# A two-layer hybrid decoder trunk on one core: layers written out, first step of each net by token tile, shorter first loads and final norm

## The chip, the core and the metric

The kernel runs on one core of a Trainium2 chip. A core has TensorE (matmuls and transposes, results in PSUM), VectorE (DVE), ScalarE (ACT), GpSimd (POOL) and a queue, SyncE (SP), that here issues nearly all DMAs. Each engine runs its own list of instructions in order and waits on semaphores for the others. The metric is the device time of one execution in microseconds.

## The reference, cut

Two layers over 256 tokens of width 1024, all in float32:

```
for l in range(2):
    x = LN1(ALPHA * x + 0.5 * (silu(x @ w_gate) * (x @ w_up)) @ w_down)   # w_gate, w_up: 1024 x 2816
    x = LN2(ALPHA * x + mixer(x))      # x @ w_in (1024 x 4864), conv, S5 scan, window attention, gates, w_out
    x = LN3(ALPHA * x + 0.5 * SwiGLU_2(x))
```

## The kernel before

All weights, about 200 MB, are read from HBM once in 93 chunks of 1 MB per layer (33 for each feed-forward net, 27 for the mixer). A chunk lands in one of three raw slots (`load`, on SP). ACT rounds it to fp32r (`split`, w_hi, L710), DVE subtracts to get the rest (`rest`, w_lo, L1056), and TensorE multiplies in three passes: hi x hi, hi x lo, lo x hi. Activations are split in the same way. A slot's raw part is free once `rest` is done, and its hi and lo parts when TensorE has used them (semaphore `used`).

The 256 tokens are two tiles of 128. `xtok` holds x by token, `xT` holds it by feature: 8 feature chunks, hi and lo. TensorE keeps PSUM banks 0 to 3 as accumulators (`acc`) of a net's output; tile 0 is in banks 0 and 1, tile 1 in 2 and 3.

A feed-forward net has 11 steps of 256 hidden columns. `project` computes a gate or an up chunk: the weights are stationary, 256 tokens move, 48 matmuls (L426 to L428). ACT applies silu, DVE multiplies (`hid`), both split it, and `accumulate` adds its product with a down chunk: 24 matmuls of 512 columns (L441). Gate and up of step i+1 run ahead of the accumulation of step i. Ahead of the first step `open_acc` writes zeros to the accumulators (L467).

Between two nets stands `norm`. When the accumulators of tile 0 are complete, DVE adds the residual (L1108), takes statistics (L1112, L1117, L1119), POOL raises the variance to -0.5 (L988) and DVE normalises (L1123). The same follows for tile 1. TensorE transposes each tile (L456, 8 transposes), ACT evacuates with gain and shift (L768; for a quarter it is DVE, L1154) and casts to hi (L762), DVE subtracts to get lo (`x_rest`, L1102). Only then can `project` start. At LN1 eight more transposes, of the scan's B and C matrices (L522, L523), stand between the two tiles' transposes, and the first mixer chunk is K/V, which is computed by token tile with x stationary (L543 to L545).

The layers are a hardware loop on every engine (`Fori(0, DEPTH)`). So the input x takes the same path as the output of a layer: gains are set to 1, and x is transposed, evacuated and split like any other. All parameter vectors are loaded by the ACT queue at the start, and SP waits for them before it loads the first weights. Behind the loop DVE and POOL multiply the normalised output by the gain and add the shift (L1442, L1444, L1038, L1040), and two stores write it.

Within an engine the order of the code is the order of the work: no scheduler moves anything.

```
with sp.Fori(0, DEPTH) as l:                       # and so on each engine
norm(l, 1, FFN0[1] - 1, 1.0); turned(l, 1)         # DVE between mixer and second net
rest(l, FFN0[1] + 1)                               # low part of the second weight chunk, behind it
```

## Time and profile before

| | |
|---|---|
| Median of 3 runs | 1194.88 us (1194.86 to 1196.68) |
| Profiled execution | 1195.63 us, span 1193.8 us |
| Busy in the span | TensorE 1145.8 us (96%), DVE 753.7 (63%), ACT 575.2 (48%), POOL 154.1 (13%) |
| Read from HBM | 203.77 MB, 172 GB/s over the span |
| Mean granted TensorE clock | 0.984 |

The span runs from the first to the last instruction. A busy time is a share of it, and says nothing of what waits for what; the timeline does.

### The profile page before, as it was taken

The numbers are of one execution on the slowest core, as the hardware profiler recorded it, in microseconds if no ns is written. First come the engines' busy times: TensorE is split into PE (matmuls) and PEld (weight loads), VectorE is DVE, ScalarE is ACT, GpSimd is POOL, SyncE is SP. The second block draws the span as 40 slices with busy tenths as digits, with TensorE's granted clock in tenths as the row PEclk, the third lists the DMA queues.
The fourth block names the chain that finished last, engine by engine and source line by source line (L and its number), as shares of the span: only waits on it lengthen the run. The fifth ranks groups of instructions, "written<-read, shape, count | busy, mean of one in ns | idle before, by whom it ended". The sixth has DMA issues, their size and how long they took to land.

```text
span 1193.8 us, 20955 instructions
## 1 busy us (share of the span) xinstructions
PE 1145.8 (96%) x8164; PEld 1082.6 (91%) x8166; DVE 753.7 (63%) x700; ACT 575.2 (48%) x652; POOL 154.1 (13%) x147
## 2 busy tenths in 40 slices
PE   5999999999999899999979999999999998999995
PEld 5999999999999799999879999989999988999994
DVE  4665447779948664544557544577897586644455
ACT  5565553863444544334356555455735435334331
POOL 2199000003000000000004950000300000000001
PEclk8999999999999899999989999999999998999998
DMA  7565567443466456556455655645445563555650
GB/s 223 181 211 189 192 200 193 155 129 117 139 178 200 153 177 190 195 176 215 139 157 178 207 176 189 232 107 177 141 135 153 174 219 126 191 178 187 197 177 35
DMA packets 176209, 205.60 MB, mean 172 GB/s; under 512 B 27012, under 2 KB 160792, under 8 KB 176152
## 3 DMA queue, kind: packets, MB, share of 16 engines
q1 hardware_dynamic: 175824, 204.76, 54.2%
q8 instruction: 36, 0.59, 0.2%
q14 instruction: 21, 0.17, 0.1%
q10 hardware_dynamic: 328, 0.08, 0.0%
HBM read 203.77 MB, written 1.05 MB: 172 GB/s over the span
## 4 chain that ended last, share of the span: by engine, by line
issue 79%; POOL 13%; PE 6%; ACT 1%; DVE 1%; POOLq 0%; ACTq 0%; DVEq 0%
POOL rot_c L1008 3%; POOL rot_s L1014 2%; POOL tp L1012 2%; POOL S L1022 2%; PE ps L428 1%; PE ps L427 1%; PE ps L426 1%; POOL tp L1010 1%; POOL tp L1004 1%; POOL tp L1006 1%; ACT S L879 1%; PE ps L606 1%; POOL rstd L988 1%; PE ps L543 0%; PE ps L544 0%
## 5 line engine op out<-in xcount | busy, mean ns | idle before, releaser
L1056 DVE TENSOR_TENSOR w_lo<-raw,w_hi 128x2048 fp32r<-128x2048 f32 x186 | 434.4, 2338 | 271.4 <-ACT w_hi L710 271.4
L426 PE MATMUL ps<-xT,w_hi 128*128 128x256 f32 x1984 | 568.1, 286 | 12.8 <-DVE xT L1102 12.8
L427 PE MATMUL ps<-xT,w_hi 128*128 128x256 f32 x1984 | 564.6, 285 | 0.0
L428 PE MATMUL ps<-xT,w_lo 128*128 128x256 f32 x1984 | 564.5, 285 | 0.0
L710 ACT CAST w_hi<-raw 128x2048 fp32r<-128x2048 f32 x186 | 353.4, 1902 | 155.1 <-PE ps L428 114.7
L426 PEld LDWEIGHTS ps<-xT,w_hi 128*128 128x128 f32 x1984 | 384.2, 194 | 17.3 <-DVE xT L1102 15.7
L427 PEld LDWEIGHTS ps<-xT,w_hi 128*128 128x128 f32 x1984 | 384.2, 194 | 1.7
L428 PEld LDWEIGHTS ps<-xT,w_lo 128*128 128x128 f32 x1984 | 383.9, 193 | 0.0
L441 PE MATMUL ps<-w_hi,rows_hi 128*128 128x512 f32 x416 | 130.8, 391 | 0.0
L441 PE MATMUL ps<-w_lo,rows_hi 128*128 128x512 f32 x416 | 130.4, 390 | 0.0
L441 PE MATMUL ps<-w_hi,rows_lo 128*128 128x512 f32 x416 | 130.2, 389 | 0.0
L988 POOL TENSOR_TENSOR rstd<-veps,mhalf 128x1 f32<-128x1 f32 x12 | 6.6, 550 | 815.3 <-DVE veps L1119 815.3
L441 PEld LDWEIGHTS ps<-w_lo,rows_hi 128*128 128x128 f32 x416 | 78.1, 188 | 16.7
L441 PEld LDWEIGHTS ps<-w_hi,rows_lo 128*128 128x128 f32 x416 | 78.1, 188 | 16.6
L721 ACT CAST rows_hi<-hid 128x512 fp32r<-128x512 f32 x44 | 27.3, 620 | 132.3 <-PE ps L441 98.2
L441 PEld LDWEIGHTS ps<-w_hi,rows_hi 128*128 128x128 f32 x416 | 75.3, 189 | 13.1
L715 ACT ACTIVATE act<-ps 128x512 f32<-128x512 f32 x44 | 26.3, 597 | 123.0 <-PE ps L428 122.9
L1069 DVE TENSOR_TENSOR rows_lo<-hid,rows_hi 128x512 fp32r<-128x512 f32 x44 | 32.7, 742 | 57.5 <-ACT rows_hi L721 57.4
L1064 DVE TENSOR_TENSOR hid<-act,ps 128x512 f32<-128x512 f32 x44 | 30.2, 687 | 49.1 <-PE ps L428 49.1
L818 ACT ACTIVATE gates<-ps 128x512 f32<-128x512 f32 x24 | 14.4, 598 | 80.6 <-PE ps L428 80.6
L768 ACT ACTIVATE xTf<-ps,ln_cur 128x128 f32<-128x128 f32 x72 | 27.0, 455 | 9.9 <-PE ps L456 9.9
L1008 POOL TENSOR_TENSOR rot_c<-tp 128x512 f32<-128x512 f32 (+6 forms) x18 | 31.7, 1759 | 1.4
(186 smaller groups left out, 930.4 us busy)
## 6 DMA issues: line engine op xcount, KB each, us to landing
raw<-in_ffn_w_gate SPq DMA_DIRECT2D x44, 1024.0 KB, 5.4
raw<-in_ffn_w_up SPq DMA_DIRECT2D x44, 1024.0 KB, 5.3
raw<-in_ffn_w_down SPq DMA_DIRECT2D x44, 1024.0 KB, 4.9
raw<-in_w_in SPq DMA_DIRECT2D x34, 1024.0 KB, 5.3
raw<-in_w_out SPq DMA_DIRECT2D x8, 1024.0 KB, 4.9
raw<-in_w_in SPq DMA_DIRECT2D x16, 256.0 KB, 4.5
raw<-in_w_br_attn SPq DMA_DIRECT2D x16, 256.0 KB, 4.6
gb<-in_ln_g SPq DMA_DIRECT2D x6, 512.0 KB, 5.3
```

The costliest lines, as they stand in the source:

```text
L426: mm(o, h[:, c, n], xT[:, c, 0, :], start=i == 0, stop=False)
L427: mm(o, h[:, c, n], xT[:, c, 1, :], start=False, stop=False)
L428: last = mm(o, w[:, c, n], xT[:, c, 0, :], start=False, stop=i == KC - 1)
L441: last = mm(acc[:, t, n, :], left[:, buf, c, tok], right[:, c, n * 512:n * 512 + 512], start=start and first and c == 0, stop=stop and lef ...
L710: nc.scalar.copy(w_hi[s][:, :], raw[s][:, :]).then_inc(hi_made.sem, 1)
L715: act_(act[:, :, :], ps[:, 4, :].rearrange("p (m t) -> p m t", m=2), ACT.Silu).then_inc(silu_made.sem, 1)
L721: nc.scalar.copy(rows_hi[:, buf], hid[:, :, :]).then_inc(h_hi.sem, 1)
L768: last = act_(xTf[:, c, t * P:t * P + P], ps[:, 6 - 2 * t + c // 4, (c % 4) * P:(c % 4 + 1) * P], ACT.Identity, scale=ln_cur[:, 2 * (norm_ ...
L1008: tt(rot_c[:, tl, n:2 * n], t0, t1, ALU.subtract).then_inc(pool_chain, 1)
L1056: tt(w_lo[s][:, :], raw[s][:, :], f32(w_hi[s][:, :]), ALU.subtract).then_inc(lo_made.sem, 1)
L1064: tt(hid[:, :, :], act[:, :, :], ps[:, 5, :].rearrange("p (m t) -> p m t", m=2), ALU.mult).then_inc(h_made.sem, 1)
L1069: tt(rows_lo[:, buf], hid[:, :, :], f32(rows_hi[:, buf]), ALU.subtract).then_inc(h_lo.sem, 1)
```

## The change

- Layers are written out in Python loops on every engine; the inner loops over steps stay.
- The first gate and up chunks of each net are computed by token tile with x stationary (`by_token`), into banks 0 and 1 and with tokens as rows: tile 0 by pairs of feature chunks, with tile 1's transposes ahead of tile 0's last pair. The first `hid` is therefore by token, and TensorE transposes it (four transposes). `open_acc` is gone: the first accumulation starts the banks.
- ACT evacuates and casts by pairs of feature chunks, DVE's `x_rest` goes by pairs too, and for tile 0 stands between the residual and statistics operations of tile 1. At the second and third norm the `rest` of the next net's second chunk (`second`) moves from behind the norm to between its tiles; in layer 0 that of the next layer's first chunk goes ahead of the norm.
- The input is cast straight from PSUM, without gains. The first loads are issued at once: tile 0 of x, half of the first weight chunk, tile 1 of x, the other half, the second chunk; the parameter vectors come behind these on SP, and their transposes move into the first net's step 1. Eight zero matmuls run ahead of the first transposes.
- In the last norm DVE does centring times gain, and then times deviation plus shift, in two operations; tile 0 is stored when it is ready, and tile 1 in two halves.

```diff
+first = ffn1_w_gate[0].rearrange("(c p) n -> p c n", p=P)
+sp.dma_start(xtok[:, 0, :], x[0, 0:P, :]).then_inc(x_landed[0], 16)
+sp.dma_start(cols(raw[0])[:, 4:KC, :], first[:, 4:KC, 0:256]).then_inc(first_landed, 16)
+sp.dma_start(xtok[:, 1, :], x[0, P:2 * P, :]).then_inc(x_landed[1], 16)
 sp.sem_inc(lo_made.sem, SLOTS)
 sp.sem_inc(used.sem, SLOTS)
...
-sp.wait_ge(small_landed, 16 * 12)
...
-    load(l, k0, columns(w_gate, l, 0))
+    if l == 0 and f == 0:
+        load(l, k0, lambda r: [(cols(r)[:, 0:4, :], first[:, 0:4, 0:256])])
+    else:
+        load(l, k0, columns(w_gate, l, 0))
...
-with sp.Fori(0, DEPTH) as l:
+for l in range(DEPTH):
...
+def by_token(l, norm, t, p, chunks):
+    pe.wait_ge(x_lo.sem, x_lo.at(l, 8 * norm + 4 * t + p + 1))
+    tok = slice(t * P, t * P + P)
+    for c in PAIRS[p]:
+        for slot, o, inc in chunks:
+            h, w = cols(w_hi[slot])[:, c, :], cols(w_lo[slot])[:, c, :]
+            mm(o, xT[:, c, 0, tok], h, start=c == UPPER_FIRST[0], stop=False, skip_group_check=True)
+            mm(o, xT[:, c, 0, tok], w, start=False, stop=False, skip_group_check=True)
+            last = mm(o, xT[:, c, 1, tok], h, start=False, stop=c == UPPER_FIRST[-1], skip_group_check=True)
+            if inc and c == UPPER_FIRST[-1]:
+                last.then_inc(used.sem, 1)
...
-def open_acc(l, n):
-    pe.wait_ge(res_made.sem, res_made.at(l, n))
+def gate_up_by_token(l, k0, norm):
+    transposes(l, norm, 0)
+    take(l, k0)
+    take(l, k0 + 1)
     for t in range(NT):
-        for h in range(2):
-            mm(acc[:, t, h, :], zero_b[:, 0:P], zero_b[:, :], start=True, stop=False,
-               skip_group_check=True)
+        part = slice(t * 256, t * 256 + 256)
+        chunks = ((0, ps[:, 0, part], t), (1, ps[:, 1, part], t))
+        for p in range(4):
+            if t == 0 and p == 3:
+                transposes(l, norm, 1)
+            by_token(l, norm, t, p, chunks)
+def gate_up_of_input():
+    pe.wait_ge(zero_made, 1)
+    for _ in range(8):
+        mm(ps[:, 1, :], zero_b[:, 0:P], zero_b[:, :], start=True, stop=True, skip_group_check=True)
+    pe.wait_ge(ident_made, 1)
+    transposes(0, -1, 0)
+    pe.wait_ge(first_lo, 1)
+    for k in range(2):
+        for t in range(NT):
+            part = slice(t * 256, t * 256 + 256)
+            for p in range(4):
+                if k == 0 and t == 0 and p == 2:
+                    transposes(0, -1, 1)
+                    take(0, 0)
+                elif k == 1 and t == 0 and p == 0:
+                    take(0, 1)
+                by_token(0, -1, t, p, ((k, ps[:, k, part], t),))
 def ffn(l, f, norm):
     k0, s0 = FFN0[f], f * STEPS
-    take(l, k0)
-    project(0, 4, l, norm)
-    take(l, k0 + 1)
-    project(1, 5)
-    def step(i):
+    if l == 0 and f == 0:
+        gate_up_of_input()
+    else:
+        gate_up_by_token(l, k0, norm)
+    def step(i, first=False):
         take(l, k0 + i * 3 - 1)
-        pe.wait_ge(silu_made.sem, silu_made.at(l, s0 + i))
+        if not first:
+            pe.wait_ge(silu_made.sem, silu_made.at(l, s0 + i))
         project(2, 4)
+        if first and l == 0 and f == 0:
+            pe.wait_ge(rows_made, 1)
+            nc.tensor.transpose(ps[:, 7, 0:N_LN], ln_rows, ident[0:N_LN, 0:N_LN])
+            nc.tensor.transpose(ps[:, 7, P:P + N_SMALL], small_rows, ident[0:N_SMALL, 0:N_SMALL]
+                                ).then_inc(pro_tp, 1)
         take(l, k0 + i * 3)
         pe.wait_ge(h_made.sem, h_made.at(l, s0 + i))
+        if first:
+            for m in range(2):
+                for t in range(NT):
+                    n = m * SEQ + t * P
+                    last = nc.tensor.transpose(ps[:, 6, n:n + P], hid[:, t, m * P:m * P + P], ident[:, :])
+            last.then_inc(hT_done.sem, 1)
         project(0, 5)
         take(l, k0 + i * 3 + 1)
         pe.wait_ge(h_lo.sem, h_lo.at(l, s0 + i))
-    with pe.Fori(1, STEPS - 1) as i:
+    step(1, True)
...
+    step(1, True)
+    accumulate(1, 0, start=True).then_inc(used.sem, 1)
+    with pe.Fori(2, STEPS - 1) as i:
...
+for l in range(DEPTH):
...
+def first_hidden_hi(l, f):
+    sc_.wait_ge(hT_done.sem, hT_done.at(l, f + 1))
+    nc.scalar.copy(rows_hi[:, 0], ps[:, 6, :].rearrange("p (m t) -> p m t", m=2)).then_inc(h_hi.sem, 1)
...
+def norm(l, norm_):
+    def evacuate(t, p, n):
+        for c in PAIRS[p]:
             last = act_(xTf[:, c, t * P:t * P + P], ps[:, 6 - 2 * t + c // 4, (c % 4) * P:(c % 4 + 1) * P],
                         ACT.Identity, scale=ln_cur[:, 2 * (norm_ % 3), c:c + 1],
                         bias=ln_cur[:, 2 * (norm_ % 3) + 1, c:c + 1])
         last.then_inc(xTf_act.sem, 1)
-        sc_.wait_ge(xTf_act.sem, xTf_act.at(l, norm_ * 3 + n))
-        x_split(slice(ks[0], ks[-1] + 1), t)
+        sc_.wait_ge(xTf_act.sem, xTf_act.at(l, norm_ * 6 + n))
+        x_split(slice(PAIRS[p][0], PAIRS[p][1] + 1), t)
     sc_.wait_ge(tp_upper.sem, tp_upper.at(l, norm_ * NT + 1))
-    evacuate(0, range(4, KC), 1)
+    evacuate(0, 0, 1)
+    evacuate(0, 1, 2)
     sc_.wait_ge(tp_made.sem, tp_made.at(l, norm_ * NT + 1))
-    evacuate(0, range(4), 2)
-    if between:
-        between()
+    evacuate(0, 2, 3)
+    evacuate(0, 3, 4)
...
+    cast(0, 1)
+    cast(0, 0)
+    sc_.wait_ge(first_landed, 16)
+    nc.scalar.copy(cols(w_hi[0])[:, 4:KC, :], cols(raw[0])[:, 4:KC, :]).then_inc(first_hi, 1)
+    sc_.wait_ge(landed[0], LANDED[0])
+    nc.scalar.copy(cols(w_hi[0])[:, 0:4, :], cols(raw[0])[:, 0:4, :]).then_inc(hi_made.sem, 1)
+    cast(1, 1)
+    cast(1, 0)
+    split(0, 1)
...
+def x_rest(l, norm_, t, p):
+    dve.wait_ge(x_hi.sem, x_hi.at(l, norm_ * 8 + 4 * t + p + 1))
+    ks, tok = slice(PAIRS[p][0], PAIRS[p][1] + 1), slice(t * P, t * P + P)
     tt(xT[:, ks, 1, tok], xTf[:, ks, tok], f32(xT[:, ks, 0, tok]), ALU.subtract).then_inc(x_lo.sem, 1)
...
+    def centred(t):
+        stt(xtok[:, t, :], xtok[:, t, :], mv[:, t, 0:1], gb[:, 0, :], ALU.subtract, ALU.mult
+            ).then_inc(dev_made, 1)
+        dve.wait_ge(dev_made, t + 1)
+        dve.wait_ge(rstd_made.sem, rstd_made.at(l, norm_ * NT + t + 1))
+    def finished(t, at):
+        stt(xtok[:, t, at], xtok[:, t, at], rstd[:, t:t + 1], gb[:, 1, at], ALU.mult, ALU.add
+            ).then_inc(out_made, 1)
     dve.wait_ge(acc_done.sem, acc_done.at(l, 2 * norm_ + 1))
...
+    if final:
+        dve.wait_ge(gb_landed.sem, gb_landed.at(DEPTH, 0))
+        centred(0)
+        finished(0, slice(0, D))
+    else:
+        normalise(0, slice(0, D))
+    def ahead(p):
+        if not final:
+            x_rest(l, norm_, 0, p)
     dve.wait_ge(acc_done.sem, acc_done.at(l, 2 * norm_ + 2))
+    if second is not None:
+        second()
     residual(1, slice(0, 1)).then_inc(dve_chain, 1)
     dve.wait_ge(dve_chain, links.next())
-    stats(1, 0)
+    if second is None:
+        stats(1, 0)
     dve.wait_ge(used.sem, used.at(l, k + 1))
     residual(1, slice(1, 2)).then_inc(res_made.sem, 1)
     dve.wait_ge(res_made.sem, res_made.at(l, norm_ * NT + 2))
+    ahead(0)
+    if second is not None:
+        stats(1, 0)
+    ahead(1)
     stats(1, 1).then_inc(dve_chain, 1)
+    ahead(2)
     deviation(1)
-    normalise(1, slice(D // 2, D))
-    normalise(1, slice(0, D // 2))
-def turned(l, norm_, between=None):
-    x_rest(l, norm_ * 4 + 1, slice(4, KC), 0)
-    x_rest(l, norm_ * 4 + 2, slice(0, 4), 0)
+    if final:
+        centred(1)
+        finished(1, slice(0, D // 2))
+        finished(1, slice(D // 2, D))
+    else:
+        ahead(3)
+        normalise(1, slice(D // 2, D))
+        normalise(1, slice(0, D // 2))
...
+    low(0, 1)
+    low(0, 0)
+    dve.wait_ge(first_hi, 1)
+    tt(cols(w_lo[0])[:, 4:KC, :], cols(raw[0])[:, 4:KC, :], f32(cols(w_hi[0])[:, 4:KC, :]), ALU.subtract
+       ).then_inc(first_lo, 1)
+    dve.wait_ge(hi_made.sem, hi_made.at(0, 1))
+    tt(cols(w_lo[0])[:, 0:4, :], cols(raw[0])[:, 0:4, :], f32(cols(w_hi[0])[:, 0:4, :]), ALU.subtract
+       ).then_inc(lo_made.sem, 1)
+    low(1, 1)
+    low(1, 0)
+    rest(0, 1)
...
-    norm(l, 1, FFN0[1] - 1, 1.0)
+    norm(l, 1, FFN0[1] - 1, 1.0, lambda: rest(l, FFN0[1] + 1))
     turned(l, 1)
-    rest(l, FFN0[1] + 1)
-    ffn(l, 1, True, lambda: scaled_back(l, 1))
-    norm(l, 2, LAYER_CHUNKS - 1, 0.5)
-    links.leave()
-dve.wait_ge(gb_landed.sem, gb_landed.at(DEPTH, 0))
-dve.wait_ge(xn_made.sem, xn_made.at(DEPTH, 0))
-for t, part in ((1, slice(0, D)), (0, slice(D // 2, D))):
-    tt(xtok[:, t, part], xtok[:, t, part], gb[:, 0, part], ALU.mult).then_inc(dve_chain, 1)
-    dve.wait_ge(dve_chain, links.next())
-    tt(xtok[:, t, part], xtok[:, t, part], gb[:, 1, part], ALU.add).then_inc(out_made[t], 1)
+    ffn(l, 1, lambda: scaled_back(l, 1))
+    if l < DEPTH - 1:
+        rest(l + 1, 0)
+        norm(l, 2, LAYER_CHUNKS - 1, 0.5, lambda: rest(l + 1, 1))
+        turned(l + 1, -1)
+    else:
+        norm(l, 2, LAYER_CHUNKS - 1, 0.5, None, True)
```

What stands in the engines' lists at three places follows. The names are those of the tiles, and "waits" names the semaphores on which an instruction waits.

DVE between mixer and second net, from the statistics of tile 1 on, before:

```order
L1112 BN_STATS bnst<-xtok 128x6 [waits dve_chain]
L1139 REGISTER_ALU
L1108 SCALAR_TENSOR_TENSOR xtok<-xtok,ps 128x512 [waits used]
L1141 REGISTER_ALU
L1112 BN_STATS bnst<-xtok 128x6 [waits res_made]
L1115 REGISTER_ALU
L1117 BN_AGGR mv<-bnst 128x2 [waits dve_chain]
L1118 REGISTER_ALU
L1119 TENSOR_SCALAR veps<-mv 128x1 [waits dve_chain]
L1123 TENSOR_SCALAR xtok<-xtok,mv,rstd 128x512 [waits rstd_made]
L1123 TENSOR_SCALAR xtok<-xtok,mv,rstd 128x512
L1102 TENSOR_TENSOR xT<-xTf,xT 128x4x128 [waits x_hi]
```

and now, from the normalisation of tile 0 on:

```order
L1167 TENSOR_SCALAR xtok<-xtok,mv,rstd 128x1024 [waits rstd_made]
L1095 TENSOR_TENSOR w_lo<-raw,w_hi 128x2048 [waits hi_made,acc_done]
L1152 SCALAR_TENSOR_TENSOR xtok<-xtok,ps 128x512
L1152 SCALAR_TENSOR_TENSOR xtok<-xtok,ps 128x512 [waits used,dve_chain]
L1146 TENSOR_TENSOR xT<-xTf,xT 128x2x128 [waits x_hi,res_made]
L1156 BN_STATS bnst<-xtok 128x6
L1146 TENSOR_TENSOR xT<-xTf,xT 128x2x128 [waits x_hi]
L1156 BN_STATS bnst<-xtok 128x6
L1146 TENSOR_TENSOR xT<-xTf,xT 128x2x128 [waits x_hi]
L1161 BN_AGGR mv<-bnst 128x2 [waits dve_chain]
L1163 TENSOR_SCALAR veps<-mv 128x1 [waits dve_chain]
L1146 TENSOR_TENSOR xT<-xTf,xT 128x2x128 [waits x_hi]
```

A `rest` (L1095) and four x_rest of half the size (L1146) have moved in among tile 1's operations. At the first norm there is no `rest` there, and both statistics wait in the same way.

TensorE at the same place, before:

```order
L456 MATMUL ps<-ident,xtok 128x128 [waits xn_made]
L456 MATMUL ps<-ident,xtok 128x128 x7
L453 REGISTER_ALU
L456 MATMUL ps<-ident,xtok 128x128 [waits xn_made]
L456 MATMUL ps<-ident,xtok 128x128 x3
L455 REGISTER_ALU
L456 MATMUL ps<-ident,xtok 128x128 [waits xn_made]
L456 MATMUL ps<-ident,xtok 128x128 x3
L467 MATMUL ps<-zero_b 128x512 [waits res_made]
L467 MATMUL ps<-zero_b 128x512 x3
```

and now, where the last six rows are the start of the first of three pairs ahead of tile 1's transposes:

```order
L489 MATMUL ps<-ident,xtok 128x128 [waits xn_made]
L489 MATMUL ps<-ident,xtok 128x128 x7
L455 MATMUL ps<-w_hi0,xT 128x256 [waits x_lo,lo_made]
L456 MATMUL ps<-w_lo0,xT 128x256
L457 MATMUL ps<-w_hi0,xT 128x256
L455 MATMUL ps<-w_hi1,xT 128x256
L456 MATMUL ps<-w_lo1,xT 128x256
L457 MATMUL ps<-w_hi1,xT 128x256
```

Matmuls of tile 0 have moved ahead of tile 1's transposes, and the zero writes are gone.

ACT at the start, before, from the wait for POOL's constants on:

```order
L800 UNCONDITIONAL_BRANCH [waits consts_made]
L800 ISA
L768 ACT_TABLE_LOAD
L768 ACTIVATE xTf<-ps,ln_cur 128x128 [waits tp_upper]
L768 ACTIVATE xTf<-ps,ln_cur 128x128 x3
```

and now:

```order
L842 ACT_TABLE_LOAD [waits tp_upper]
L842 CAST xT<-ps 128x4x128
L842 CAST xT<-ps 128x4x128 [waits tp_made]
L848 CAST w_hi<-raw 128x1024 [waits first_landed]
L850 CAST w_hi<-raw 128x1024 [waits landed0]
L842 CAST xT<-ps 128x4x128 [waits tp_upper]
L842 CAST xT<-ps 128x4x128 [waits tp_made]
L753 CAST w_hi<-raw 128x2048 [waits used,landed1]
```

The wait for the first transposes has moved from the first evacuation onto the table load, and the cast of the second weight chunk stands behind those of tile 1.

## Rows read from the trace of the kernel before

**Rows 1.** Windows: stretch; busy us per engine (x instructions); clock; DMA.

```profile
405.50:408.50 3.00, 3.00 (x15) 3.00 (x16) 3.00 (x3) 2.72 (x2) 0.00 (x0) 0.50 0.03 5
410.00:590.00 180.00, 180.00 (x1280) 170.14 (x1280) 90.02 (x57) 69.65 (x53) 0.00 (x0) 1.00 0.59 192
```

**Rows 2.** Timeline of TensorE, start: start us, us, instruction, idle before.

```profile
8.39 3.62 PE L456 MATMUL ps<-ident,xtok 128*128 128x128 f32 x16
...
18.56 0.58 PE L426 MATMUL ps<-xT,w_hi 128*128 128x256 f32 x1 [5.20 <-DVE xT L1102]
...
43.57 0.28 PE L428 MATMUL ps<-xT,w_lo 128*128 128x256 f32 x1
43.69 0.40 PE L441 MATMUL ps<-w_hi,rows_hi 128*128 128x512 f32 x1
```

**Rows 3.** Timeline of TensorE, first turn of layer 0.

```profile
207.57 1.03 PE L456 MATMUL ps<-ident,xtok 128*128 128x128 f32 x8
...
211.44 1.00 PE L456 MATMUL ps<-ident,xtok 128*128 128x128 f32 x7 [1.96 <-DVE xtok L1123]
...
218.35 0.28 PE L426 MATMUL ps<-xT,w_hi 128*128 128x256 f32 x1
```

**Rows 4.** Timeline of TensorE, second turn of layer 0.

```profile
397.62 1.04 PE L456 MATMUL ps<-ident,xtok 128*128 128x128 f32 x8
401.39 1.47 PE L456 MATMUL ps<-ident,xtok 128*128 128x128 f32 x8 [2.74 <-DVE xtok L1123]
...
405.31 0.58 PE L426 MATMUL ps<-xT,w_hi 128*128 128x256 f32 x1 [0.73 <-DVE xT L1102]
...
429.98 0.63 PE L441 MATMUL ps<-w_hi,rows_hi 128*128 128x512 f32 x2
```

**Rows 5.** Timeline of TensorE, from layer 0 to layer 1.

```profile
593.71 1.03 PE L456 MATMUL ps<-ident,xtok 128*128 128x128 f32 x8
...
605.50 0.58 PE L426 MATMUL ps<-xT,w_hi 128*128 128x256 f32 x1 [6.04 <-DVE xT L1102]
...
630.69 0.63 PE L441 MATMUL ps<-w_hi,rows_hi 128*128 128x512 f32 x2
```

**Rows 6.** Timeline of DVE, end of the kernel.

```profile
1178.42 0.15 DVE L1119 TENSOR_SCALAR veps<-mv 128x1 f32<-128x1 f32 x1
...
1183.90 2.88 DVE L1123 TENSOR_SCALAR xtok<-xtok,mv,rstd 128x512 f32<-128x512 f32 x2 [0.66 <-POOL rstd L988]
...
1190.01 0.69 DVE L1444 TENSOR_TENSOR xtok<-xtok,gb 128x512 f32<-128x512 f32 x1
```

**Rows 7.** Timeline of DVE, second turn of layer 0.

```profile
396.86 0.68 DVE L1108 SCALAR_TENSOR_TENSOR xtok<-xtok,ps 128x512 f32<-128x512 f32 x1
...
399.98 0.15 DVE L1119 TENSOR_SCALAR veps<-mv 128x1 f32<-128x1 f32 x1
400.79 1.00 DVE L1123 TENSOR_SCALAR xtok<-xtok,mv,rstd 128x512 f32<-128x512 f32 x2 [0.66 <-POOL rstd L988]
```

**Rows 8.** Groups by form: busy us, mean ns of one, idle before and releaser.

```profile
L1102 DVE TENSOR_TENSOR xT<-xTf,xT 128x512 fp32r<-128x512 f32 x24 | 15.9, 688 | 6.8 <-ACT xT L762 4.0 <-issue 2.2
...
L762 ACT CAST xT<-xTf 128x512 fp32r<-128x512 f32 x24 | 14.7, 618 | 0.8 <-DVE xTf L1154 0.3
```

**Rows 9.** Timeline of DVE, behind the first turn of layer 0.

```profile
215.73 4.49 DVE L1056 TENSOR_TENSOR w_lo<-raw,w_hi 128x2048 fp32r<-128x2048 f32 x2
```

**Rows 10.** Timeline of ACT, second turn of layer 0.

```profile
395.09 1.92 ACT L710 CAST w_hi<-raw 128x2048 fp32r<-128x2048 f32 x1 [5.73 <-PE ps L441]
398.26 1.51 ACT L768 ACTIVATE xTf<-ps,ln_cur 128x128 f32<-128x128 f32 x4 [1.25 <-PE ps L456]
```

**Rows 11.** DMA issues: count, KB each, median us to landing.

```profile
xtok<-in_x SPq DMA_DIRECT2D x1, 1024.0 KB, 5.1
```

**Rows 12.** Timeline of DVE, first instruction of layer 1.

```profile
600.08 1.29 DVE L1102 TENSOR_TENSOR xT<-xTf,xT 128x512 fp32r<-128x512 f32 x2 [2.19 <-issue]
```

**Rows 13.** Timeline of ACT, first instruction.

```profile
7.86 1.28 ACT L768 ACT_TABLE_LOAD   x1 [7.86 <-POOLq L976]
```

354 lines of the change are left out of this document (172 added, 182 removed).

## The prediction

> **What bounds the kernel now.** I read the busy time of each engine by stretch first: between 410 and 590 us TensorE is busy for 180.00 us of 180.00 [rows 1]. Inside a feed-forward net nothing waits for a load or a cast, so no edit there can gain, and every added TensorE instruction costs its full time. What is left lies where TensorE stands. I walked TensorE's timeline for starts later than the end before them, and found the start, three turns per layer where a layer norm stands between two nets (I call them the first turn, first net to mixer; the second, mixer to second net; and the layer turn), and the tail behind the last matmul.
>
> I measure each place by a distance that other work does not touch: from the first transpose of token tile 0 (or from zero) to the first matmul into the accumulators of the net (L441), which is 96 gate/up matmuls and then 96 more later.
> Start: 43.69 us [rows 2]. First turn: 218.35 - 207.57 = 10.78, to the first matmul behind K/V [rows 3]. Second turn: 429.98 - 397.62 = 32.36 [rows 4]. Layer turn: 630.69 - 593.71 = 36.98 [rows 5]. Tail: the last DVE instruction ends at 1190.70, the store behind it ends the span at 1193.8 [rows 6].
>
> Two things make these long. First, the chain: DVE normalises tile 1 (400.79), TensorE stands for 2.74 us before its transposes and again for x_lo. At the layer turn it stands for 6.04 us more, because DVE starts L1102 after 2.19 us of "issue" (its jump back to the loop's head) and puts `rest(l, 0)` in between [rows 5, 12]. Second, the clock: after such waits the clock is granted at half of 2.4 GHz (405.5 to 408.5: 0.50, 15 matmuls in 3 us) [rows 1]. At full clock two matmuls start 0.12 us apart [rows 2], so 192 take 23.0 us; the second turn's took 429.98 - 405.31 = 24.7 and the layer turn's 25.2. The clock costs 1.7 and 2.2 us there.
>
> **The change, part by part.** Durations: an x_rest of 512 columns takes 688 ns, a cast of 512 takes 618 ns [rows 8], two w_lo of 2048 columns 4.49 us [rows 9], 2.29 each less an overlap of 0.08. That is 1.04 ns per column and a fixed part of 0.16; a piece of 256 is 0.42 us, and starts 0.08 before the one ahead of it ends (two of 512 took 1.29) [rows 12]. An ACT pair (two evacuations and a cast of 256) is 0.83 + 0.40 less overlap, 1.14 us per pair; four evacuations took 1.51 [rows 10].
>
> *Second turn*, with 0 at tile 0's first transpose (397.62). ACT starts at 0.64 and delivers x_hi at 1.88, 3.02, 4.16, 5.30. DVE was ready for tile 1's residual at -0.76 [rows 7]. Now it first does `rest` of the second weight chunk; its cast is at -2.53 to -0.61 (395.09) [rows 10], so `rest` ends DVE-wise at 1.64. Two residuals of 0.71 give 3.06, then x_rest 0 done at 3.48, stats, x_rest 1 at 4.44, stats, x_rest 2 at 5.40, aggregate, veps, x_rest 3 at 6.07, POOL's power 6.4, normalised halves at 6.9 and 7.4. So tile 1 is 3.2 us later than before, but TensorE has work: 1.04 of transposes, idle to 3.54 (2.5 us), three pairs of 12 matmuls at 1.44 to 7.86, tile 1's transposes to 8.74, pair 3 to 10.2, then tile 1's first x_lo (transposed 8.5, ACT 1.24, DVE) at 10.3, four pairs to 16.05. Then the next 96 matmuls, 11.51, and four new transposes of `hid`, 0.44: 28.0 against 32.36, so -4.4, twice: -8.7. The removed zero writes lay in the same waits and are in this difference. The chunk behind (w_lo of k0+2) is ready at about 15.8, just in time: cover of 0.3 us.
>
> *Layer turn*: the same sequence, since the loop's jump and `rest(l, 0)` are gone from between; `rest` of chunk 0 goes into a DVE gap of 3 us ahead of the norm. 28.1 against 36.98: -8.9.
>
> *First turn*: K/V was by token before, so little is won, and this kernel has no `second` there. Its waits for x_hi hold DVE: x_rest 1 must wait for ACT's second pair (3.02 after the first transpose), and x_rest 3 for 5.30. Tile 1's first half is normalised at 6.2 instead of 3.87, where the idle 1.96 ended (211.44) [rows 3]. TensorE's eight B/C transposes, 0.87, which filled that wait, now stand behind tile 1's. K/V then ends at 12.3 instead of 10.78. And `rest` of the next chunk, which follows the four x_rest on DVE, ends at 13.0; before, it was done at 215.73 + 2.29 = 218.0, 0.3 us ahead of its use [rows 3, 9]. I take 13.0: +2.2, twice: +4.4.
>
> *Start*: zero matmuls keep TensorE busy from 1.3. I take them at half clock, as the 16 first transposes took 3.62 us, 0.21 each, against 1.04 for eight later [rows 2, 4]. They end at 4.8. Half of x, 512 KB, is there by then: 1 MB took 5.1 from 0.75 [rows 11]. Tile 0's upper transposes are ready at 5.85. The table load of 1.28 us [rows 13], which had run under the wait for consts, now carries the wait for the transposes, so 7.2; two casts of x and half a weight chunk (1.05), 9.3; DVE's half (1.22), 10.5. First real matmul at 10.5 instead of 18.56. But then the second chunk rules: ACT casts it only after tile 1's x (14 to 15.6), DVE ends at 18 to 19.8, and its 48 matmuls end at 24 to 25.6. I take 25.0, plus 11.51, 0.44, and 0.3 for the two parameter transposes: 37.2 against 43.69, -6.5 (-4.5 to -8).
>
> *Tail*: DVE's tile-0 veps starts at 1178.42 [rows 6]. Centring (1024 columns by the per-column price, start to start 1.25) and finishing (1.14) bring it to 1180.9; the tile-1 chain residual to veps is 399.98 - 396.86 = 3.12 [rows 7], 1184.0; then 0.08 + 1.25 + 0.61 + 0.68: last end 1186.6 instead of 1190.70. -4.1 (-3.4 to -4.4: the store is half as large). POOL's two operations, under which two normalisations had taken 2.88 us [rows 6] instead of 1.00 [rows 7], go.
>
> *Unrolling*, the constants' order and the static waits: nothing, under TensorE's steady work; the loop's one visible price is in the layer turn.
>
> Sum: -6.5 + 4.4 - 8.7 - 8.9 - 4.1 = -23.8 us. The profiled execution took 1195.63 (span 1193.8), so 1171.8; the median of the runs, 1194.88, lies 0.75 below it: **1171.1 us**.
>
> The Trainium skill has a rule against pairs: VectorE: DVE Perf Modes, section on the TRN2 errata, says that each SBUF-source instruction pays a fixed cost and asks for tiles of at least 512 elements; its fp32 formula, (N+151)/0.96 ns, gives an estimate of 424 ns for 256. My rows give the same duration but a start-to-start of 0.34 us. Were the pieces not overlapped, as the page's sentence on the bubble between instructions suggests, four per turn would add 0.3 us, and the sum would be 1172.7.
>
> **Rivals.**
> (a) The clock falls at the turns all the same. For: at the second turn it fell after 2.74 us of idle, and 2.5 are left; against: at the first turn 1.96 us did not bring it down [rows 3, 4]. Price 1.7 us at each of three places and 1 to 2 at the start: 1177 to 1178.
> (b) The first turn costs nothing, because DVE gets its x_hi sooner than I reckon: -4.4, 1166.7. Against: ACT's price per evacuation is measured.
> (c) By-token order does not help: TensorE's first pair waits until tile 1 is normalised, because DVE's queue holds the low part behind `rest` and the statistics. Then the second turn gains only the zero writes (1 us), the layer turn the jump and the inserted `rest` (5), start and tail as above: 1194.9 - 6.5 + 4.4 - 2 - 5 - 4.1 = 1181.7. DVE's rows put x_rest 0 ahead of both statistics, so it would need ACT to be 3 us late.
> (d) Slower: the unrolled program. TensorE's list grows from 2010 to 4259 rows. The one row that shows a program fetched from elsewhere is DVE's 2.19 us of issue at the loop's jump [rows 12]. If straight code paid such a stall on TensorE's path, 11 of them (23.8 / 2.19) eat the gain; one for each of the 12 nets, mixer halves and turns would give 1197. Against: 180 us without a gap, through straight and looped code alike [rows 1]. The Trainium skill (Advanced Engine Details and Errata, ISA Cache) describes an instruction cache of only two lines per engine; by it a long straight program would be fetched once per line, as the body of the old loop already was, and no row shows a stall from that.
>
> **How the numbers follow.** Forecast (1167 to 1175) 0.62; (a), in part or whole, 0.18; (b) or a shorter start 0.12; (c) 0.05; (d) 0.02; no change 0.01. The low end, 1166, is (b) with a little; the high end, 1178, is (a) whole. Together they leave out somewhat less than 2 in 10. A measurement of this kernel tells 0.2% (2.4 us) from no change: faster 0.96, same 0.01, slower 0.03.
>
> **What would show it.** First matmul of L455 before 11 us; first accumulate near 37; at the second and layer turns about 28 us from first transpose to first accumulate, with one idle of 2.5 us; at the first turn 13 us and an idle of about 0.8 before the Q chunk, released by DVE's w_lo; DVE's end some 4 us earlier. It is wrong if half-clock stretches stay behind the turns, or if the first x_rest starts more than 4 us after the first transpose.

## The result, and the profile after

The changed kernel takes 1178.59 us (median of 4 runs, 1178.00 to 1179.31) against 1194.87 us of the kernel before on the same chip: a ratio of 0.9866, 95% interval 0.9845 to 0.9887. The prediction was 1171.1 us with a range of 1166 to 1178. The sign and the order of the work were right, the pace of TensorE behind the turns was not; about a third of the gain did not come, and the time lies just outside the range.

The profiled execution took 1179.31 us, its span 1177.5 us (1193.8 before). By section, from the same events in both traces:

| section | distance before | distance after | change | predicted |
|---|---|---|---|---|
| start, to first accumulate | 43.69 | 37.82 | -5.87 | -6.5 |
| first turn to the Q chunk, two layers | 10.78 each | 13.07, 13.06 | +4.9 by the second turn | +4.4 |
| second turn, two layers | 32.36, 32.41 | 29.85, 29.84 | -5.1 | -8.7 |
| layer turn | 36.98 | 29.86 | -7.1, of which 0.5 is lost behind it | -8.9 |
| first accumulate of the last net to the end | 176.77 | 173.38 | -3.4 | -4.1 |

The stretch from the first accumulate to the first turn is 0.15 us shorter too, and the whole is -16.2 (spans of 1193.76 and 1177.53 with one more digit). Timeline of TensorE in the changed kernel: the start, the first turn and the second turn of layer 0, the layer turn (to be held against [rows 2 to 5]).

```profile
1.32 3.60 PE L512 MATMUL ps<-zero_b 128*128 128x512 bf16 x8 [1.32 <-POOL zero_b L1017]
4.71 1.38 PE L489 MATMUL ps<-ident,xtok 128*128 128x128 f32 x8
10.36 0.58 PE L455 MATMUL ps<-w_hi,xT 128*128 128x256 f32 x1 [4.27 <-DVE w_lo L1248]
...
19.86 0.39 PE L455 MATMUL ps<-w_hi,xT 128*128 128x256 f32 x1 [0.23 <-DVE w_lo L1095]
...
37.82 0.63 PE L471 MATMUL ps<-w_hi,rows_hi 128*128 128x512 f32 x2
...
204.10 0.35 PE L455 MATMUL ps<-w_hi,xT 128*128 128x256 f32 x1 [1.52 <-DVE xT L1146]
...
214.62 0.39 PE L442 MATMUL ps<-xT,w_hi 128*128 128x256 f32 x1 [0.46 <-DVE w_lo L1095]
...
394.05 1.04 PE L489 MATMUL ps<-ident,xtok 128*128 128x128 f32 x8
397.81 0.44 PE L455 MATMUL ps<-w_hi,xT 128*128 128x256 f32 x1 [2.72 <-DVE xT L1146]
...
403.69 1.04 PE L489 MATMUL ps<-ident,xtok 128*128 128x128 f32 x8
...
423.90 0.63 PE L471 MATMUL ps<-w_hi,rows_hi 128*128 128x512 f32 x2
...
587.63 1.03 PE L489 MATMUL ps<-ident,xtok 128*128 128x128 f32 x8
591.39 0.36 PE L455 MATMUL ps<-w_hi,xT 128*128 128x256 f32 x1 [2.72 <-DVE xT L1146]
...
617.49 0.63 PE L471 MATMUL ps<-w_hi,rows_hi 128*128 128x512 f32 x2
...
634.97 0.73 PE L471 MATMUL ps<-w_hi,rows_hi 128*128 128x512 f32 x2 [0.34 <-DVE w_lo L1095]
```

The forecast's shape is there: one idle of 2.72 us at the second turn (2.5 predicted), tile 1's transposes without a wait, an idle of 0.46 ahead of the Q chunk, released by DVE's w_lo. What the forecast did not have is the slow pace of the matmuls behind that idle. Windows behind the idle of the layer turn (columns as in [rows 1]):

```profile
592.00:593.00 1.00, 1.00 (x8) 1.00 (x8) 1.00 (x3) 0.93 (x3) 0.00 (x0) 0.75 0.97 401
593.00:594.00 1.00, 1.00 (x6) 1.00 (x6) 0.71 (x4) 0.00 (x0) 0.51 (x1) 0.50 0.84 344
594.00:595.00 1.00, 1.00 (x7) 1.00 (x6) 0.82 (x2) 0.00 (x0) 0.15 (x1) 0.50 0.00 0
595.00:596.00 1.00, 1.00 (x7) 1.00 (x7) 0.19 (x1) 0.00 (x0) 0.00 (x0) 0.55 0.00 0
596.00:597.00 1.00, 1.00 (x10) 1.00 (x10) 0.00 (x0) 0.00 (x0) 0.00 (x0) 1.00 0.61 63
```

The clock is granted at 0.50 of 2.4 GHz for some 3.4 us (592.5 to 595.9), and matmuls start 0.21 us apart instead of 0.12. In 3.4 us that is some 16 matmuls, each 0.094 us late: 1.5 us.

DVE and POOL at the second turn of layer 0 and at the end (against [rows 6, 7]):

```profile
393.59 2.29 DVE L1095 TENSOR_TENSOR w_lo<-raw,w_hi 128x2048 fp32r<-128x2048 f32 x1 [0.22 <-ACT w_hi L753]
...
397.24 0.42 DVE L1146 TENSOR_TENSOR xT<-xTf,xT 128x256 fp32r<-128x256 f32 x1
...
400.60 1.00 DVE L1167 TENSOR_SCALAR xtok<-xtok,mv,rstd 128x512 f32<-128x512 f32 x2 [0.44 <-POOL rstd L1037]
...
1165.65 1.28 DVE L1172 SCALAR_TENSOR_TENSOR xtok<-xtok,mv,gb 128x1024 f32<-128x1024 f32 x1
1165.82 1.52 POOL L1037 TENSOR_TENSOR rstd<-veps,mhalf 128x1 f32<-128x1 f32 x1 [184.99 <-DVE veps L1163]
1167.45 1.28 DVE L1178 SCALAR_TENSOR_TENSOR xtok<-xtok,rstd,gb 128x1024 f32<-128x1024 f32 x1 [0.52 <-POOL rstd L1037]
...
1173.64 1.42 DVE L1178 SCALAR_TENSOR_TENSOR xtok<-xtok,rstd,gb 128x512 f32<-128x512 f32 x2 [0.52 <-POOL rstd L1037]
```

At the second turn `rest` of the second chunk runs first, then come the two residuals of tile 1 (1.40 us), tile 0's first x_rest, and at 400.60 tile 1's normalisation. At the end DVE waits 0.52 us in each tile for POOL's power, which takes 1.52 us there.

### The profile page after: what moved, and what is told of

It is laid out like the page before. It is cut to its first block, busy times and chain, and to the rows that moved or that the text cites. A ratio compares the mean times of both kernels' runs of the same rounds, so it can differ in the third digit from the quotient of the medians.

```text
span 1177.5 us, 19863 instructions
## 1 busy us (share of the span) xinstructions
PE 1146.0 (97%) x8174; PEld 1082.3 (92%) x8174; DVE 748.1 (64%) x713; ACT 571.9 (49%) x659; POOL 149.7 (13%) x141
## 4 chain that ended last, share of the span: by engine, by line
PE 83%; DVE 9%; ACT 5%; issue 3%; POOL 0%; POOLq 0%; DVEq 0%; ACTq 0%
PE ps L471 23%; PE ps L442 16%; PE ps L444 16%; PE ps L443 16%; DVE w_lo L1095 3%; ACT w_hi L753 2%; PE ps L455 2%; PE ps L457 1%; PE ps L456 1%; PE ps L717 1%; PE ps L718 1%; PE ps L719 1%; DVE td L1379 1%; DVE bu L1399 1%; DVE tp L1380 1%
## 5 line engine op out<-in xcount | busy, mean ns | idle before, releaser
L1095 DVE TENSOR_TENSOR w_lo<-raw,w_hi 128x2048 fp32r<-128x2048 f32 x185 | 432.3, 2339 | 248.6 <-ACT w_hi L753 248.4
L442 PE MATMUL ps<-xT,w_hi 128*128 128x256 f32 x1856 | 528.3, 285 | 0.9 <-DVE w_lo L1095 0.9
L444 PE MATMUL ps<-xT,w_lo 128*128 128x256 f32 x1856 | 525.2, 283 | 0.0
L443 PE MATMUL ps<-xT,w_hi 128*128 128x256 f32 x1856 | 525.1, 283 | 0.0
L442 PEld LDWEIGHTS ps<-xT,w_hi 128*128 128x128 f32 x1856 | 356.0, 192 | 3.0 <-DVE w_lo L1095 1.3
L443 PEld LDWEIGHTS ps<-xT,w_hi 128*128 128x128 f32 x1856 | 356.1, 192 | 1.7
L444 PEld LDWEIGHTS ps<-xT,w_lo 128*128 128x128 f32 x1856 | 356.0, 192 | 0.0
L769 ACT CAST rows_hi<-hid 128x512 fp32r<-128x512 f32 x40 | 24.8, 620 | 117.1 <-PE ps L471 100.7
L455 PE MATMUL ps<-w_hi,xT 128*128 128x256 f32 x160 | 50.6, 316 | 17.8 <-DVE xT L1146 13.2
L1113 DVE TENSOR_TENSOR rows_lo<-hid,rows_hi 128x512 fp32r<-128x512 f32 x40 | 29.6, 741 | 56.8 <-ACT rows_hi L769 56.3
L455 PEld LDWEIGHTS ps<-w_hi,xT 128*128 128x128 f32 x160 | 33.4, 209 | 21.8 <-issue 12.3
```

Source lines behind the costliest of these rows:

```text
L442: mm(o, h[:, c, n], xT[:, c, 0, :], start=i == 0, stop=False)
L443: mm(o, h[:, c, n], xT[:, c, 1, :], start=False, stop=False)
L444: last = mm(o, w[:, c, n], xT[:, c, 0, :], start=False, stop=i == KC - 1)
L455: mm(o, xT[:, c, 0, tok], h, start=c == UPPER_FIRST[0], stop=False, skip_group_check=True)
L769: nc.scalar.copy(rows_hi[:, buf], hid[:, :, :]).then_inc(h_hi.sem, 1)
L1095: tt(w_lo[s][:, :], raw[s][:, :], f32(w_hi[s][:, :]), ALU.subtract).then_inc(lo_made.sem, 1)
```

## Experiments

The open questions: is it the clock that keeps the second and layer turns 1.5 us above the forecast; what does it cost at the start; what lengthens the first turn; what do the order of the pairs, the moved `rest` and the unrolling bring by themselves; and why does DVE wait in the tail. Distances below are from the first transpose of tile 0 to the first accumulate, unless another end is named. A zero matmul multiplies zeros into a bank whose content nobody reads; it only keeps TensorE at work. Where one profiled run is given, there is no second time to hold it against, and the reading rests on distances inside its trace: the eight traces that have the changed kernel's start unedited, its own among them, reach the first accumulate at 37.4 to 38.05 us.

### Zero matmuls in the idle of the second and layer turns

```
 transposes(l, norm, 0)
+for _ in range(11):
+    mm(ps[:, 0, :], zero_b[:, 0:P], zero_b[:, :], start=True, stop=True)
 take(l, k0)
```

> The changed kernel with 11 zero matmuls (512 columns, into bank 0, which is free there) behind tile 0's transposes at the second turns and the layer turn, so that TensorE does not stand for the 2.72 us until the first x_lo. Theory (the clock falls at these turns all the same): the zeros take about 2.4 us at full clock, the granted clock stays at 1 there, the distance from the first transpose to the first accumulate goes from 29.85 to about 28.1 us at all three turns, and the time from 1178.6 to about 1173.5 us. Rival (the queue of DVE and ACT behind the turn sets the distance, not the clock): the clock stays full but the distance stays within 0.3 us of 29.85, and the time at 1178.6.

1174.93 us, ratio to before 0.9823 [0.9810, 0.9836]; span 1173.1. TensorE's timeline:

```profile
395.24 2.32 PE L499 MATMUL ps<-zero_b 128*128 128x512 bf16 x10
397.91 0.36 PE L455 MATMUL ps<-w_hi,xT 128*128 128x256 f32 x1 [0.35 <-DVE xT L1148]
...
422.51 0.63 PE L471 MATMUL ps<-w_hi,rows_hi 128*128 128x512 f32 x2
```

The first pair starts 3.76 us after the first transpose (394.15), as without the zeros, so DVE and ACT did nothing sooner. All three distances fall from 29.85 to 28.35 us (28.36, 28.34, 28.36; I had expected 28.1), and the span by 4.4. The rival, a queue that sets the distance, is out. The clock costs 1.5 us at each of these turns. (Of the 11 zeros the trace has records of 10, of the 4 below records of 3.)

With 4 zeros instead of 11:

> The changed kernel with 4 zero matmuls instead of 11 behind tile 0's transposes at the second and layer turns: TensorE then stands for 1.8 us instead of 2.72. The rows so far: idles of 1.51 to 1.96 us at the first turn kept the full clock, one of 2.02 lost it once, those of 2.72 lost it ten times of eleven. Theory (shortening the idle is enough, it need not be filled): full clock and a distance of 28.35 us at all three turns, span 1173.1 as with 11 zeros. Rival (the whole stretch must be busy): 29.8 us at the turns where the clock falls, span up to 1177.5.

One profiled run, span 1172.7:

```profile
394.83 0.81 PE L499 MATMUL ps<-zero_b 128*128 128x512 bf16 x3
397.50 0.36 PE L455 MATMUL ps<-w_hi,xT 128*128 128x256 f32 x1 [1.86 <-DVE xT L1148]
```

28.34, 28.35 and 28.35 us: four were enough in these three passages. But what decides is not the length of the idle alone. (The counts in the expectation were off: 1.52 us had lost the clock once by then, and 2.72 us eleven times of twelve.) Over the changed kernel and all its profiled variants in which TensorE stood for 2.72 or 2.73 us at these turns, the clock fell in 12 of 15 passages; in the 3 others the distance was 28.35 without any zeros. At the new first turn's idle of 1.52 us it fell in 2 passages of 16 (layer 0 of the run with start zeros, layer 1 of the run without warm-up: 13.77 and 13.88 us instead of 13.06). With the idle filled to 0.36 us or less it fell in none of 18. What else decides stays open.

### Zero matmuls at the start

```
 transposes(0, -1, 0)
+for _ in range(10):
+    mm(ps[:, 1, :], zero_b[:, 0:P], zero_b[:, :], start=True, stop=True)
 pe.wait_ge(first_lo, 1)
```

> The changed kernel with 10 more zero matmuls behind the first transposes at the start, which fill the 4.27 us in which TensorE waits for the first weight chunk's low part. Theory (the half clock at the start is covered by the wait for the second chunk): the first 48 matmuls run at 0.12 instead of 0.21 us each, but TensorE then waits longer for the second chunk's low part, whose 19.8 us is set by ACT and DVE; the first accumulate stays within 0.3 us of 37.82. Rival (the half clock at the start costs its full time): the first accumulate at 36.3 us or sooner, the span 1.5 us shorter.

One profiled run, span 1174.5. TensorE, and DVE's low part of the second chunk, here and (last row) in the changed kernel:

```profile
5.91 2.32 PE L516 MATMUL ps<-zero_b 128*128 128x512 bf16 x10
10.35 0.38 PE L455 MATMUL ps<-w_hi,xT 128*128 128x256 f32 x1 [2.12 <-DVE w_lo L1250]
...
35.77 0.63 PE L471 MATMUL ps<-w_hi,rows_hi 128*128 128x512 f32 x2
...
15.47 2.29 DVE L1097 TENSOR_TENSOR w_lo<-raw,w_hi 128x2048 fp32r<-128x2048 f32 x1 [0.93 <-ACT w_hi L755]
```

```profile
17.51 2.29 DVE L1095 TENSOR_TENSOR w_lo<-raw,w_hi 128x2048 fp32r<-128x2048 f32 x1 [1.05 <-ACT w_hi L753]
```

My theory fell and the rival stands: the first accumulate comes at 35.77 instead of 37.82, 2.05 us sooner, with the first real matmul at the same 10.35. I had taken the second chunk's 19.8 us for fixed by ACT and DVE. It is not: ACT casts it behind tile 1 of x, tile 1's transposes stand behind two pairs of matmuls on TensorE, and these ran at half pace. With them at full pace the low part is ready at 17.76, and not at 19.80.

The eight zeros that the change itself put ahead of the first transposes:

> The changed kernel without the 8 zero matmuls ahead of the first transposes. Theory (they let the first transposes run at full speed): tile 0's transposes, 8 in 1.38 us, take 1.9, the chain ACT, DVE, first matmul starts 0.5 us later, and the first accumulate is at 38.4 instead of 37.8. Rival (they do nothing: the transposes wait for x's landing, and their speed is what it is): 37.8 within 0.2.

One profiled run, span 1175.3:

```profile
4.61 1.94 PE L489 MATMUL ps<-ident,xtok 128*128 128x128 f32 x8 [4.61 <-DMA xtok<-in_x]
5.79 1.28 ACT L840 ACT_TABLE_LOAD   x1 [5.79 <-PE ps L489]
10.41 0.58 PE L455 MATMUL ps<-w_hi,xT 128*128 128x256 f32 x1 [3.86 <-DVE w_lo L1246]
```

The transposes take 1.94 us instead of 1.38, but the first real matmul starts at 10.41 and the first accumulate is at 37.85, as with them. They do nothing for the time by themselves, and the trace shows why. ACT's table load is released by the first four transposes, at 5.79 us here and at 5.74 with the zeros: those four run 0.21 us apart in both, and start 0.10 us sooner without zeros ahead of them. Only the last four are faster with the zeros (0.11 apart), and ACT, busy with the table load of 1.28 us, does not yet need them. Behind the idle that follows the matmuls run at half pace in both. (The span is shorter because the clock did not fall at two of the three later turns.)

### The first turn in the order of before

```
 transposes(l, 0, 0)
-by_token of K/V, tile 0; transposes(l, 0, 1); B/C transposes; by_token, tile 1
+B/C transposes; transposes(l, 0, 1); by_token of K/V, tiles 0 and 1
-                    if not final:                 # ahead(p), on DVE
+                    if not final and norm_:
     normalise(1, slice(0, D // 2))
+    if norm_ == 0: x_rest(l, 0, 0, p) for p in range(4)
```

> The changed kernel with the first turn in the order of the kernel before: DVE does tile 0's four x_rest behind the normalisation of tile 1, and TensorE does the B/C transposes, then tile 1's transposes, then K/V of both tiles. The pairs in ACT's evacuation stay. Theory (the interleaved x_rest hold tile 1's normalisation, because each waits for ACT's pair): tile 1 is normalised about 3.9 us after the first transpose, K/V ends at 10.6, and the Q chunk's w_lo, still last on DVE, at 11.1; so the distance goes from 13.07 to 11.1 us in both layers and the time from 1178.6 to 1174.7 us. Rival (ACT's evacuation by pairs is what made it longer): the distance stays above 12.5 us, the time above 1177.5.

1175.39 us, ratio 0.9824 [0.9810, 0.9837]; span 1174.2. Layer 0 takes 10.99 us to the Q chunk (13.07 before this edit, 11.1 expected). Layer 1 takes 12.14. TensorE's timeline there, and last a row of DVE at the first turn of the changed kernel:

```profile
783.50 1.21 PE L489 MATMUL ps<-ident,xtok 128*128 128x128 f32 x8 [2.02 <-DVE xtok L1166]
...
784.72 0.42 PE L456 MATMUL ps<-w_lo,xT 128*128 128x256 f32 x1
784.94 0.42 PE L457 MATMUL ps<-w_hi,xT 128*128 128x256 f32 x1
```

```profile
204.61 0.43 DVE L1146 TENSOR_TENSOR xT<-xTf,xT 128x256 fp32r<-128x256 f32 x1 [0.65 <-ACT xT L810]
```

The steps are 0.21 us apart until 787.7: this turn met the half clock after an idle of 2.02 us, while layer 0 kept full clock after 1.89. So the interleaving did cost the 2.1 us, and ACT's pairs at most 0.2 (the rival asked for 12.5 and more in both layers): 10.99 is within 0.21 of the kernel before [rows 3]. The edit moves work on DVE and on TensorE at once, and the traces tell the shares: in the changed kernel DVE stands 0.74, 0.65 and 0.42 us for ACT's pairs and normalises tile 1 from 5.70 us after the first transpose, here from 3.19; tile 1's transposes start at 6.65 and 3.79 us. Of these 2.86 us 2.51 are DVE's, and 0.35 the pairs that stand ahead of the transposes on TensorE.

### The moved `rest` put back

```
-norm(l, 1, FFN0[1] - 1, 1.0, lambda: rest(l, FFN0[1] + 1))
+norm(l, 1, FFN0[1] - 1, 1.0)
+rest(l, FFN0[1] + 1)
 turned(l, 1)                      # and the same at the layer turn
```

> The changed kernel with the low part of the second weight chunk back behind the norm's normalisation (as before the change, ahead of DVE's share of the evacuation) at the second and layer turns. The forecast's reading: tile 1 is normalised 2.2 us sooner, but the first by-token pair needs both chunks and now waits for the low part: it starts about 7.4 us after the first transpose instead of 3.76, and the distance becomes about 32 us instead of 29.85; three times +2.2, time 1185 us. Rival (tile 1's normalisation is what counts, so the move bought nothing): the distance stays at 29.85 or falls, time 1178 or less.

1197.03 us, ratio 1.0009 [1.0000, 1.0018]: with this one statement moved back the whole gain is gone. (One operation follows it: without `rest` in `norm` the first statistics of tile 1 stand ahead of its second residual, as they did before.) TensorE, and last DVE:

```profile
394.25 1.04 PE L489 MATMUL ps<-ident,xtok 128*128 128x128 f32 x8
403.25 0.55 PE L455 MATMUL ps<-w_hi,xT 128*128 128x256 f32 x1 [7.95 <-DVE w_lo L1095]
...
410.22 1.04 PE L489 MATMUL ps<-ident,xtok 128*128 128x128 f32 x8
...
411.30 0.73 DVE L1229 TENSOR_SCALAR xTf<-ps,ln_cur 128x128 f32<-128x128 f32 x2 [8.15 <-PE ps L489]
```

The distances are 36.18, 35.34 and 35.50 us, 5.8 us longer on the mean where I expected 2.2. The first pair waits until 9.0 us after the first transpose, not 7.4: DVE's four x_rest, each behind its ACT pair, and both normalisations stand ahead of `rest`. And nothing of the 5.2 us by which the first pair is late is made up (the rest of the 5.8 is half clock: 4.0 to 5.9 us of it behind the start of the first pair, not 3.4): tile 1's transposes, ready at 401.0, stand behind three pairs until 410.22, and DVE is idle for 8.15 us meanwhile. I had let the later steps catch up.

### Tile 1's transposes ahead of all pairs

```
+transposes(l, norm, 1)
 take(l, k0)
 take(l, k0 + 1)
 ...
-        if t == 0 and p == 3:
-            transposes(l, norm, 1)
```

> The changed kernel with tile 1's transposes ahead of all by-token pairs at the second and layer turns, so that nothing of tile 0 runs under the wait for tile 1's normalisation (the third rival of the prediction, built). Theory (the gain at these turns is the work that fills this wait): TensorE stands until 7.5 us after the first transpose, tile 0's pairs start at 8.4, tile 1's end at 19.9, and with 12 us of the next matmuls and 1.5 for the clock the distance is 33.5 us instead of 29.85; three turns, time 1189.5 us. Rival (the pairs by token are faster by themselves, or ACT's evacuation of tile 1 is what rules): the distance below 31 us.

1190.10 us, ratio 0.9958 [0.9945, 0.9971]; distances 33.18, 33.63 and 33.05 us, as expected (33.5):

```profile
401.12 1.97 PE L489 MATMUL ps<-ident,xtok 128*128 128x128 f32 x8 [6.12 <-DVE xtok L1166]
```

TensorE stands 6.12 us until tile 1 is normalised. The gain of the second turns over the kernel before (32.4) needs the pairs of tile 0 inside this wait; matmuls by token alone would have lost there. At the layer turn 33.63 is still 3.4 us below the 36.98 of before, where the loop's jump has gone as well.

### Layers written out, nothing else

The kernel before with `for l in range(DEPTH)` in place of `Fori(0, DEPTH)` on every engine.

> The kernel before with one part of the change alone: the layers written out on every engine. The forecast's reading: only the layer turn gains, since DVE's 2.19 us of issue at the jump goes; its distance of 36.98 us becomes 34.8, or 33 if the shorter wait also spares some of the clock; all other distances (first turn 10.78, second 32.36) stay; time 1192.7 us, 1191 at the least. Rival (straight code has to be fetched and stalls the engines): the distances of the turns grow, and the time is above 1195.

1193.36 us, ratio 0.9981 [0.9972, 0.9990]; span 1191.5. The layer turn takes 34.36 us, with TensorE's idle ahead of its first matmul 4.05 us instead of 6.04 [rows 5]:

```profile
9.49 1.28 ACT L766 ACT_TABLE_LOAD   x1 [9.49 <-PE ps L454]
...
605.12 0.55 PE L424 MATMUL ps<-xT,w_hi 128*128 128x256 f32 x1 [4.05 <-DVE xT L1100]
```

The first and second turns of layer 0 stay (10.76 and 32.42). The second turn of layer 1 was 1.35 us shorter with the same idle of 2.72 ahead of tile 1's transposes, because its real matmuls ran 0.12 us apart from the first on. The start was 1.5 us longer (first accumulate at 45.16), which I had not expected. In the kernel before, ACT's table load ran from 7.86 us, under the wait for POOL's constants [rows 13]; written out, it stands behind the wait for the first transposes and runs from 9.49. ACT's first evacuation starts 1.30 us later for it, and TensorE's first matmul 1.4. In the changed kernel the load stands in the same place, 5.74 to 7.02 us, and ACT's first cast follows at 7.03; what it would bring to have it out of the way no run here shows. There is no new gap of TensorE in the straight code. Of the 2.62 us that the layer turn lost, 1.99 are the shorter idle, and 0.63 are that fewer matmuls behind it met the half clock (3.3 us of it, not 4.7).

### The tail: power first, then centring

```
 def centred(t):
+    dve.wait_ge(rstd_made.sem, rstd_made.at(l, norm_ * NT + t + 1))
     stt(xtok[:, t, :], xtok[:, t, :], mv[:, t, 0:1], gb[:, 0, :], SUBTRACT, MULT)
-    dve.wait_ge(rstd_made.sem, ...)
```

> The changed kernel with the wait for POOL's power ahead of the centring instead of behind it, in the last norm, so that no large DVE operation runs beside the power. Theory (POOL's power is slowed by DVE's operation on SBUF beside it): the power takes 0.55 to 0.66 us instead of 1.52; the centring starts that much later, and the end of the last store moves by less than 0.3 us either way, since the hidden time given up (1.28 us beside) is about what the contention cost. Rival (the power is slow there for another reason, its first operation after long idle): it takes 1.5 us again, and the tail is 1.3 us longer in each tile.

One profiled run, span 1177.6 (1177.5 in the changed kernel). POOL and DVE:

```profile
1165.31 0.55 POOL L1037 TENSOR_TENSOR rstd<-veps,mhalf 128x1 f32<-128x1 f32 x1 [184.98 <-DVE veps L1163]
1165.97 1.28 DVE L1173 SCALAR_TENSOR_TENSOR xtok<-xtok,mv,gb 128x1024 f32<-128x1024 f32 x1 [0.74 <-POOL rstd L1037]
```

The same power takes 0.55 us when no large DVE operation runs beside it: the 1.52 is contention, not a first operation after idle. The second power, at 1171.85, takes 0.55 as well. From DVE's first residual of the last norm to its last end the tail takes 13.04 us, and 12.42 or 12.43 in all eleven other traces that have this tail: 0.6 longer (I allowed 0.3). Half a microsecond of waiting beside is still cheaper than the whole power in front.

The Trainium skill (SBUF — State Buffer, section SBUF: two separate sides) describes this as an exclusive lock: a DVE operation with two SBUF inputs and a GpSimd one that reads SBUF do not run together, the later one waits for the end. By that rule the power would run from 1166.93, the centring's end, and the trace agrees in the end, if not in the start that it records (1165.82): the power ends at 1167.34, 0.41 behind the centring, and alone it takes 0.55.

### Together

All zeros (11 at the second and layer turns, 8 in the first turn's idle) and the first turn in the order of before:

> The changed kernel with the zero matmuls at the second and layer turns, the first turn in the order of the kernel before, and 8 zero matmuls in that turn's idle of 1.9 to 2.0 us ahead of tile 1's transposes. Theory (the parts add up, and the half clock behind layer 1's first turn, which cost 1.1 us when that turn was changed alone, goes too): first turn 11.0 us in both layers instead of 13.07, second and layer turns 28.35 instead of 29.85; span 1177.5 - 4.15 - 4.5 = 1168.9 us, time 1170.3 us. Rival (the gains overlap, or the zeros at the first turn delay the transposes): span above 1170.5.

1170.46 us, ratio 0.9792 [0.9779, 0.9806]; span 1168.4. First turns 10.99 and 11.00, the others 28.34, 28.35, 28.34. The parts add to within 0.5 us. With 12 zeros at the start as well:

> The kernel with zeros at all turns and the old first turn, and 12 zeros at the start. Theory (the parts add): start as in the run with start zeros, first accumulate at 35.8, everything else as in the kernel with the parts together: span 1168.4 - 2.0 = 1166.3, time 1168.4. Rival (the start's gain is lost at the first net's later steps): span 1168.4.

1168.70 us, ratio 0.9776 [0.9762, 0.9789]; span 1166.4, first accumulate 35.39. And with one x_rest moved:

```
 residual(1, slice(0, 1))
+ahead(0)                        # second and layer turns
 residual(1, slice(1, 2))
-ahead(0)
```

> Everything of the kernel with zeros at all turns and the old first turn, 12 zeros at the start, and at the second and layer turns tile 0's first x_rest between the two residual halves of tile 1 instead of behind them, with 9 zeros instead of 11. Theory (the first pair's start, 3.76 us after the first transpose, is DVE's two residuals; with the x_rest ahead of the second it is 3.1): TensorE gains 0.65 us there, but the next weight chunk's low part, ready 15.9 us after the first transpose, then lets it wait, so that 0.3 us a turn is left: distance 28.05 us instead of 28.35, 0.9 us of span less than the kernel without this edit (1166.3), 1165.4. Rival (tile 1 gets later by the x_rest's 0.34 and the next stall eats all): within 0.2 us of the kernel without it.

1167.03 us, ratio 0.9761 [0.9747, 0.9775]; span 1165.2, 12.3 us below that of the changed kernel. The turn (first transpose 390.06):

```profile
392.53 0.42 DVE L1151 TENSOR_TENSOR xT<-xTf,xT 128x256 fp32r<-128x256 f32 x1
393.10 0.35 PE L455 MATMUL ps<-w_hi,xT 128*128 128x256 f32 x1
...
417.84 0.63 PE L471 MATMUL ps<-w_hi,rows_hi 128*128 128x512 f32 x2
```

27.78 us in all three, 0.57 less than without the edit, where I expected 0.3: of the 0.72 us by which the pairs start sooner 0.57 are kept. The low part of the next chunk, which I had as the next bound at 15.9 us after the first transpose, came 0.57 us sooner too (15.34).

## Why the prediction was wrong

**The step that failed** is the pace behind the second and layer turns. The forecast counted 192 matmuls at 0.12 us each behind an idle of 2.5 us, and held the half clock apart as rival (a), with a chance of 0.18. The change leaves TensorE an idle of 2.72 us at the same place, nearly that of [rows 4] (2.74), behind which the clock had fallen at both second turns of the kernel before (not behind the same idle at its layer turn); it fell again in all three places, and half-clock stretches behind the turns were one of the prediction's own signs of being wrong. The argument against, that 1.96 us had not brought it down [rows 3], spoke of a shorter idle at another place. Filling the idle alone gave 1.5 us a turn, 4.5 of the 7.5 us that are missing; I had priced it at 1.7. My sum without the clock, 28.0 and 28.1, was good to 0.35 us: the kernel with zeros has 28.35.

**Start**: -5.9 instead of -6.5. Full pace was assumed from 10.5 us on, where the half clock costs 2.05 us. That the miss is only 0.6 is luck: I had put the end of the second chunk's matmuls at 25.0 within bounds of 24 to 25.6, and it came at 25.72; at the full pace that I had assumed it comes at 23.67. The first matmul (10.5 predicted, 10.36 measured) and its chain were right.

**First turn**: right, and the best-worked term: 13.0 predicted, 13.07 measured, with the named idle (0.8 predicted, 0.46 measured, as K/V ended at 12.6 and not at 12.3). The next turn came another 0.16 later than that, 4.9 for both layers instead of 4.4. The order of before gives 2.1 us a layer back, so rival (b) is out.

**Second turn, layer turn**: the order was right step by step (x_rest 0 done at 3.48 predicted, 3.61 measured; normalisation from 6.4, measured 6.55). Rival (c) is out by the trace: the first pair starts at 397.81, 2.8 us ahead of tile 1's normalisation at 400.60. Its consequence, pairs behind tile 1, was built with the transposes and measures 33.3 us, but there TensorE's order makes it and not DVE's queue; with DVE's queue as the cause (`rest` put back) it is 35.7. The jump's 2.19 us was real: with only the layers written out the layer turn is 2.62 shorter. A further 0.34 idle at 634.97 in layer 1 was not foreseen: DVE's parameter work and `scaled_back` keep it from the low parts until 631.4.

**Tail**: -3.4 instead of -4.1, and two errors stand against each other in it. DVE's last end came 2.8 us sooner, not 4.1 (15.22 to 12.42 us from the first residual): 1.04 of the 1.3 are the two waits of 0.52 for a power that I took at its unhindered length. The store behind it, which I had only in the range, gave 0.6 back (3.06 to 2.47 us from DVE's last end to the end of the span).

**Unrolling** at nothing but the jump was mis-sized too: by itself it costs 1.5 us at the start, the table load behind a wait. My start term had this load, so the sum does not miss it.

**The 0.3 us for small pieces**: three x_rest of 256 columns in a row take 1.10 us, one alone 0.42, so they overlap by 0.08 as my rows said. The extra time that the prediction worked out by the Trainium skill (VectorE: DVE Perf Modes, section on the TRN2 errata) does not show. Rival (d) is out: the kernel with only its layers written out is not slower (0.9981), and TensorE has no gap there beside those of the kernel before. That the 2.19 us of issue were a fetch of the program no run shows; they went with the jump.

The terms that missed: second turns 3.6, layer turn 2.3, start 0.5 (with the 0.15 behind it), first turns 0.5, tail 0.7: 7.6 us of span, 7.5 in the medians. The clock is 4.5 of them at the turns; filling the idle at the start as well gave 2.05.

## What to carry to other kernels

When a change shortens a wait but does not remove it, take the clock behind the wait from the row that has the same idle at the same place, and do not count on full pace unless the idle is filled; zero matmuls into a bank that the next start overwrites filled it here at no cost that the spans show. With tiles normalised one behind the other, put whatever the first real matmul needs (here the low part of a weight chunk) ahead of the second tile's work, because here a delay of 5.2 us of the first matmul was passed on whole to everything queued behind it. Ahead of interleaving work into a chain, ask whether each piece has its input: the same interleaving stood without a wait at the second and layer turns, where DVE had `rest` to do first, and lost 2.1 us at the first turns. And when a loop is written out, look at where ACT's table load comes to stand.

## What the runs showed of the hardware

- The same idle does not always have the same effect: after 2.72 or 2.73 us at one place the clock fell 12 times of 15, after 1.52 us 2 times of 16. Each second or layer turn is 28.35 or 29.6 to 29.85 us long for this alone (the run without warm-up has two of the one and one of the other), so single profiles of variants are compared turn by turn, not by their spans.
- At the start the granted clock in the profile does not tell the pace. In the changed kernel it reads 1.00 between 1 and 4 us (first row), where eight zero matmuls take 3.60 us, 0.45 each; at the turns ten take 2.32. In the run without warm-up it reads 1.00 from 12 to 14 us with 12 matmuls in 2 us, in the run with start zeros 1.00 with 20 (second and third row, windows). In the changed kernel the same stretch reads 0.50, with 12 matmuls. Only the steps between matmuls tell the pace there.

```profile
1.00:4.00 3.00, 2.68 (x7) 1.03 (x8) 0.00 (x0) 0.00 (x0) 2.58 (x7) 1.00 0.71 214
```

```profile
12.00:14.00 2.00, 2.00 (x12) 2.00 (x11) 0.00 (x0) 0.00 (x0) 0.00 (x0) 1.00 1.06 260
```

```profile
12.00:14.00 2.00, 2.00 (x20) 2.00 (x19) 0.74 (x2) 1.43 (x3) 0.00 (x0) 1.00 1.06 260
```

- A power of one element per partition takes 0.55 us on POOL, and 1.52 beside a DVE operation on two SBUF operands of 1024 columns (1.28 us).
